# Block sizes 8 and 16 of the mixer's triangular inverse: from 64x64 to 32x32 TensorE tiles

## What is computed

```python
sa = jnp.einsum('bhvk,bhk->bhv', S, -kk_t)
S = (S * w_t[:, :, None, :]
     + sa[..., None] * (kk_t * a_t)[:, :, None, :]
     + v_t[..., None] * k_t[:, :, None, :])
y = jnp.einsum('bhvk,bhk->bhv', S, r_t)
```

## Time and profile before

| | |
|---|---|
| median of 3 runs | 2969.92 us (2968.96 to 2973.3) |
| profiled execution, span from first to last instruction | 2963.8 us |
| profiled execution, its own device time | not among the times given |
| mean granted TensorE clock | 0.993 of full speed |
| TensorE busy with matmuls / weight loads | 2899.2 us / 2474.9 us |
| VectorE / ScalarE / GpSimd busy | 1594.7 / 1000.5 / 1489.8 us |
| cross products L1920 and merge products L1931 | 2,560 matmul records each |

### The profile page before, as it was taken

The page is one execution under the profiler, slowest core; times in us unless marked ns, Lnnn a source line. Parts: engine busy times, 40 slices in busy tenths (PEclk is TensorE's granted clock), DMA queues, the critical chain, the costliest instruction groups (busy, mean ns, idle before and its releaser), DMA issues. The chain is left out here.

```text
span 2963.8 us, 56296 instructions
## 1 busy us (share of the span) xinstructions
PE 2899.2 (98%) x23690; PEld 2474.9 (84%) x23690; DVE 1594.7 (54%) x2059; ACT 1000.5 (34%) x1740; POOL 1489.8 (50%) x1073
## 2 busy tenths in 40 slices
PE   8999999999999999999999999999999999999998
PEld 7888888888888879987888888887998788888887
DVE  7331634267777732329766654544233966664453
ACT  4122211245545432325333332232232533332222
POOL 4554544356666545266554533555427555543254
PEclk9999999989999999999999999999999999999999
DMA  4533455412223231112333356344111233336632
GB/s 160 183 114 96 126 167 183 146 50 61 65 57 80 71 100 43 43 50 76 115 119 140 128 192 223 142 175 156 42 46 49 85 114 135 138 111 238 230 142 85
DMA packets 175988, 346.65 MB, mean 117 GB/s; under 512 B 47233, under 2 KB 104705, under 8 KB 170113
## 3 DMA queue, kind: packets, MB, share of 16 engines
q1 hardware_dynamic: 175744, 343.16, 34.0%
HBM read 240.34 MB, written 102.76 MB: 116 GB/s over the span
## 5 line engine op out<-in xcount | busy, mean ns | idle before, releaser
L820 POOL TENSOR_TENSOR w_lo<-w_raw,w_hi 128x512 fp32r<-128x512 f32 x232 | 333.6, 1462 | 504.5 <-ACT w_hi L1124 501.0
L1679 PE MATMUL ps<-a_hi,w_hi 128*128 128x512 f32 x1140 | 445.3, 391 | 10.4 <-DVE a_lo L2396 10.0
L1679 PE MATMUL ps<-a_lo,w_hi 128*128 128x512 f32 x1140 | 444.3, 390 | 0.0
L1679 PE MATMUL ps<-a_hi,w_lo 128*128 128x512 f32 x1140 | 351.5, 390 | 0.0
L1124 ACT ACTIVATE w_hi<-w_raw 128x512 fp32r<-128x512 f32 x228 | 129.9, 623 | 625.5 <-PE ps L1679 474.7
L2216 PE MATMUL ps<-a_hi,w_hi 128*128 128x512 f32 x800 | 312.4, 391 | 11.5 <-ACT u_t L1499 4.9
L2216 PE MATMUL ps<-a_lo,w_hi 128*128 128x512 f32 x800 | 311.3, 389 | 0.0
L2216 PE MATMUL ps<-a_hi,w_lo 128*128 128x512 f32 x800 | 311.3, 389 | 0.0
L1679 PEld LDWEIGHTS ps<-a_hi,w_hi 128*128 128x128 f32 x1140 | 214.5, 188 | 55.0 <-DVE a_lo L2396 10.0
L1679 PEld LDWEIGHTS ps<-a_hi,w_lo 128*128 128x128 f32 x1140 | 214.3, 188 | 44.8
L1679 PEld LDWEIGHTS ps<-a_lo,w_hi 128*128 128x128 f32 x1140 | 214.5, 188 | 44.2 <-issue 0.2
(11 more groups left out here) (379 smaller groups left out, 6429.3 us busy)
## 6 DMA issues: line engine op xcount, KB each, us to landing
w_raw<-in_weights SPq DMA_DIRECT2D x228, 512.0 KB, 4.1
hidden<-hid SPq DMA_DIRECT2D x44, 1024.0 KB, 3.8
zT<-z_out SPq DMA_DIRECT2D x44, 512.0 KB, 3.3
a_hi<-hidden SPq DMA_DIRECT2D x44, 512.0 KB, 8.3
a_lo<-hidden SPq DMA_DIRECT2D x44, 512.0 KB, 9.4
w_raw<-kvw SPq DMA_DIRECT2D x32, 512.0 KB, 3.3
suv<-zT SPq DMA_DIRECT2D x16, 512.0 KB, 4.7
x<-in_xT SPq DMA_DIRECT2D x16, 512.0 KB, 6.0
```

What stands on the lines that cost most here:

```text
L820: pool.tensor_tensor(low_t[:, part, :], w_raw[:, u, part, :], high[:, part, :].bitcast(F32), ALU.subtract).then_inc(S["w_lo_done"], 1)
L1679: mm = pe.matmul(to[:, nb, 0:w], wt[:, k, :], r[:, k, nb * w:(nb + 1) * w], start=(k == 0 and r is hi_in and wt is high), stop=(k == kn - ...
```

## The change

For block sizes 8 and 16, each lane's product is divided into its two 32x32 diagonal blocks. A product of 64 stationary rows and columns with 32 moving columns becomes two products of 32 rows and 32 columns with 16 moving columns each, on rows 0, 32, 64 and 96, so on four diagonal tiles of the array. The parts of PSUM outside the diagonal blocks are no longer written at these sizes. Sizes 2, 4 and 32 keep their form, and so do the other engines' instructions, the order and the semaphores.

```diff
+            def blocks_of(a, b):
+
+                if b not in (8, 16):
+                    return [(lane(a), 0, C)]
+                return [(slice(a * RN + d, a * RN + d + C // 2), d, C // 2) for d in (0, C // 2)]
+
             def cross(n, par, lv):
...
                     for mh, e, a in by_tile():
-                        t_u = inv_t[lane(a), g, 2 * e + mh, :].rearrange("p (n two b) -> p n two b", two=2, b=b)[:, :, 0, :]
-                        mm = pe.matmul(unit(a, g, 2 * L + e * C + mh * 32, 32), atrb[par][lane(a), e, 2 * mh + g, 0, :], t_u,
-                                       start=True, stop=True)
+                        for rows, at, w in blocks_of(a, b):
+                            t_u = inv_t[rows, g, 2 * e + mh, at:at + w].rearrange("p (n two b) -> p n two b", two=2, b=b)[:, :, 0, :]
+                            mm = pe.matmul(ps[rows, g, 2 * L + e * C + mh * 32 + at // 2:2 * L + e * C + mh * 32 + (at + w) // 2],
+                                           atrb[par][rows, e, 2 * mh + g, 0, at:at + w], t_u, start=True, stop=True)
                     mm.then_inc(S["x_ps"], 1)
...
             def merge(n, par, lv):
...
                     for mh, e, a in by_tile():
-                        u_u = inv[par][lane(a), e, 2 * mh + g, :].rearrange("p (n two b) -> p n two b", two=2, b=b)[:, :, 1, :]
-                        mm = pe.matmul(unit(a, g, e * C + mh * 32, 32), xm[lane(a), e, g, mh, :], u_u, start=True, stop=True)
+                        for rows, at, w in blocks_of(a, b):
+                            u_u = inv[par][rows, e, 2 * mh + g, at:at + w].rearrange("p (n two b) -> p n two b", two=2, b=b)[:, :, 1, :]
+                            mm = pe.matmul(ps[rows, g, e * C + mh * 32 + at // 2:e * C + mh * 32 + (at + w) // 2],
+                                           xm[rows, e, g, mh, at:at + w], u_u, start=True, stop=True)
                     mm.then_inc(S["tu_ps"], 1)
```

## The result

| | before | changed |
|---|---|---|
| first measurement, median (6 runs each) | 2968.81 us (2967.63 to 2973.3) | 2982.8 us (2969.55 to 2990.84) |
| ratio, 95% interval | | 1.0042 [1.0029, 1.0055] |
| second measurement | 2969.67 us (30 runs, 2966.32 to 2975.65) | 2982.25 us (7 runs, 2969.37 to 2993.64) |
| ratio, 95% interval | | 1.0030 [1.0014, 1.0047] |
| profiled execution | 2963.8 us span | 2969.55 us, span 2966.9 |

The change made the kernel slower by 0.3 to 0.4%, and its executions now differ by 21 and 24 us in the two measurements, where those of before differ by 6 and 9. That spread is the first clue. The first profile is of the fastest of the six executions, so one has to keep in mind that it shows the least of the damage.

A forecast was written before the change was run, and what follows sets the result against it. The prediction took TensorE to bound the kernel, with ScalarE limiting the touched stretch. Gains of 9.4 us less 2.4 us for instructions gave 7.0 us less, 2962.9 us from 2969.92; range 2956 to 2980.

The forecast's parts named there:

- The pace of a record: Touched size-8 and size-16 products: 8.0 ns a record on four tiles, 0.51 us a product instead of 0.93.
- rival one: A record's price is an issue cost, not set by columns: 14.4 ns, about 2974 (0.15); 29 ns, 60 us more (0.04).
- rival four: 32-row products not spread over four tiles but run on two, 16 ns each: 6 us slower; chance 0.03.
- ScalarE's cap: Size-8 cross to key_scales: ScalarE's v_tok limits a steady group's gain to 0.53 us, not 1.7.
- both parts: Faster products (part one) as limited by what is late next (part two): 9.4 us less over all groups.
- The instructions: 4,096 more TensorE instructions make more packet waits in the mixer's dense stretches: 2.4 us lost, bounds 0 and 13.
- Rival two: Instruction supply becomes the bound from size-8 cross to last output product: 24 us, net +15, 2985; chance 0.10.
- A small reading: Profiled span 2963.8 us against the runs' median 2969.92: 6.1 us taken as lying around the span, unchanged after.

The follow-up runs named there:

- half_records: Changed kernel with half of the 32x32 products at sizes 8 and 16 left out, on two of four diagonal tiles: 2965.73 us, ratio 0.9988.
- quarter_records: half_records with also the mh = 1 heads' products at sizes 8 and 16 left out, 16 records a product: 2976.22 us, ratio 1.0022.
- merge16_only: Kernel before, complete computation, with the 32x32 form for the size-16 merge alone: 2967.42 us, ratio 0.9995.
- the two filled kernels: half_records and the complete changed kernel, each with every group's bonus product computed twice: 2961.98 us and 2975.87 us.
- the filler: Each group's bonus sums computed twice into the same place, one more full 128x128 product; on half_records 2961.98 us, ratio 0.9967.
- cross8_only: Kernel before, complete computation, with the 32x32 form for the size-8 cross alone: 2965.35 us, ratio 0.9985; measured again 2964.79 us, ratio 0.9981.
- after_filled: Complete changed kernel with each group's bonus product computed twice: 2975.87 us, ratio 1.0020.
- before_filled: Kernel before the change with each group's bonus product computed twice, as a control: 2981.79 us, ratio 1.0035.

## Why the prediction was wrong

The forecast was 7 us less, with 2980 as the upper end. The changed kernel took 2983. By its steps:

- **The pace of a record.** Forecast 8.0 ns and 0.51 us a product. From a product's start to the next line's it is 0.70 us; less the 0.13 that the change of line took before (1.06 less 0.93), 0.57 us or 8.9 ns a record. It saves 0.36 us instead of 0.42. Nearly right, and with it the reading that a tile's turn follows the stationary columns. (On two tiles, in half_records, it is 0.61 less 0.13 for 32 records, 15 ns each, so 30 ns a tile, where the line through the old rows gave 32; with four tiles in turn a tile's share is 36.) The 14.4, 25 and 29 ns of rival one are out, and so is rival four.
- **ScalarE's cap.** Forecast: the stretch to key_scales falls from 8.02 to 7.5 us, with a visible wait for v_tok. It is 7.47, the wait is there, and quarter_records and merge16_only show the cap apart from the rest. The sum of 9.4 us for both parts is 9.8 in half_records, at full clock.
- **The instructions.** Forecast 2.4 us, bounds 0 and 13. Measured 7.0, the changed kernel against half_records at full clock, and 11.3 between the two filled kernels. The mechanism was right and its size was off by three. I scaled today's waits as "three quarters of today's sum again", counted on ScalarE's wait to hide what is late in the touched stretch, and expected the new waits in the dense part behind it. But half of them (5.8 of 12.0 us) lie in the touched stretch itself, which now uses 39 records a us instead of 20. The densest place of the kernel did not become denser. What reserve a stretch needs was not measured. With this term alone the kernel would still be some 1 to 3 us faster.
- **The step that failed** is one that the prediction did not have: that the granted clock stays at 2.4 GHz in the mixer. It read 1.00 in the row of 100 us there and left it at that. The change took array work away (a touched product has a quarter of the multiplications that it had) and added waits, and the clock gave way: 27 us more at 1.2 GHz in a mean execution, 13.4 us. This is what turned a gain of 2.8 into a loss of 10.6 in the mean span (12.6 and 14.0 in the medians). In the Trainium skill, TensorE: Matmul & The Clock Gate ("What's actually happening") says that a hardware monitor sets the clock by how busy TensorE has been. The runs here agree: half_records and quarter_records, with less work on the array, had 14 and 28 us more at half speed than before, and the filler brought half_records back to 45 us.
- **Rival two** gave 2985 by instruction supply alone and a chance of 0.10. The number was near and the reason was not: supply costs 7 of its 24 us.
- **A small reading**, without effect on the forecast: I took 6.1 us as what lies around the span. The executions on record have 1.7 to 3.4 us there; the 6.1 compared one execution's span with the median of others.

What stays open is how the falls start. In the two profiles of the changed kernel the falls shown come right behind a late packet. But late packets do not suffice: the profiles of cross8_only and after_filled have about as many (22 and 25, against 21 and 27), and the clock of their mixers is 1.00, though their longest are 1.0 and 1.2 us, and those of the changed kernel 1.6 and 1.9. The kernel before has a single one of 1.5 us (L1903 in the earlier trace rows), and its mixer is at 1.00 too. And they are not needed: the fall shown of quarter_records comes behind waits for VectorE and ScalarE. Whether it is the sparse form of the products or the waiting that it opens which counts, no run separates. That the "issue" waits are late packets is inferred from their distance of one packet and from the runs that change the number of instructions; the packets' arrival itself was not measured.

## What to carry to other kernels

Replacing a product by more and smaller ones has three prices beside its own time: the instructions have to be there (look at how many more are used in the stretch that you change, not at the average of the stage), another engine's list may cap the gain (look for the wait that is hidden today and ends just before), and the array's clock can fall when dense work is taken away and waits come in its place. Where a gain is capped, change only the product ahead of the capping engine's idle time: one of the four products here gave more than all four. When the executions of a kernel spread wider than before, compare their granted clocks before anything else.

## What the runs showed of the hardware

- With 64 or 128 stationary columns a tile takes a new fp32 record every 58 or 111 ns, with 32 columns about every 30 ns on two tiles (half_records) and 36 on four, which is 8.9 ns a record in all. At 64 stationary columns 32 or 64 moving columns made no difference to that.
- TensorE's program came in packets of 256 instructions, and the waits that nothing else explains stand one packet apart where they follow each other closely (3.3 to 3.8 us). The same pace passed without a wait elsewhere (325 instructions in 3.30 us in the kernel before).
- Waits for packets of up to 1.2 us did not by themselves lower the clock: 15.2 us of "issue" waits in the mixer of after_filled, granted clock 1.00.
- Additional dense work on TensorE (0.85 us a group by before_filled's trace) made a kernel 3.8 us faster, and the clock in the mixer stayed at 1.00 where it had been 0.97; leaving work out made one 10 us slower (quarter_records against half_records).
